# Recurrent branch of a two-block network: gate tiles ahead of its levels, eight pieces a level, banks and tile order of its own

## The reference, cut to what matters

```python
y_a = hgrn2_mixer(hq, hf, hi, hg, lb_all[l], hgrn_norm[l])
y_b = pool_mixer(pz, pool_w[l], pool_scale[l])
y_c = dsa_mixer(sq, sk, sv, iq, ik, iw)
y_m = mem_attention(mq, mk, mv)
merged = None
for bi, y in enumerate((y_a, y_b, y_c, y_m)):
    term = jax.nn.sigmoid(u @ w_gate[l, bi]) * (y @ w_branch[l, bi])
    merged = term if merged is None else merged + term
h = h + rms_norm(merged @ w_out[l], norm_mix_post[l])
```

## Time and profile before

| | us |
|---|---|
| median of 3 runs | 2456.65 (2456.44 to 2456.81) |
| profiled execution | 2457.71, of which the span of the core 2455.9 |
| PE busy | 2274.6 (93% of the span) |
| DVE, ACT, POOL busy | 1263.6, 895.2, 368.3 |
| PE's share of the chain that ended last | 81% |
| mean granted clock of TensorE | 0.957 of full |

### The profile page before, as it was taken

The page is one execution under the profiler, slowest core; times in us unless marked ns, Lnnn a source line. Parts: engine busy times, 40 slices in busy tenths (PEclk is TensorE's granted clock), DMA queues, the critical chain, the costliest instruction groups (busy, mean ns, idle before and its releaser), DMA issues.

```text
span 2455.9 us, 28046 instructions
## 1 busy us (share of the span) xinstructions
PE 2274.6 (93%) x10190; PEld 1767.6 (72%) x10192; DVE 1263.6 (51%) x1966; ACT 895.2 (36%) x1479; POOL 368.3 (15%) x228
## 2 busy tenths in 40 slices
PE   7879799999999999899999888999969897999998
PEld 5646588888776676688888676467658675888886
DVE  4466553243464444642443664268569558443344
ACT  3444443143244453431332453322343233332333
POOL 0000420001320002400003500133022164000001
PEclk9999999999999999999999989879989898999999
DMA  5012133333233232233332332123211131333322
GB/s 163 17 36 65 52 86 103 102 94 96 67 93 107 69 86 69 69 102 103 92 97 81 91 90 71 35 62 98 74 39 56 43 99 52 104 88 107 95 70 77
DMA packets 360224, 196.43 MB, mean 80 GB/s; under 512 B 12575, under 2 KB 355372, under 8 KB 360124
## 3 DMA queue, kind: packets, MB, share of 16 engines
q1 hardware_dynamic: 360124, 195.10, 27.8%
HBM read 192.93 MB, written 2.14 MB: 79 GB/s over the span
## 4 chain that ended last, share of the span: by engine, by line
PE 81%; DVE 10%; ACT 4%; issue 2%; POOL 1%; SPq 1%; DMA 1%; DVEq 0%; ACTq 0%; POOLq 0%
PE PB L393 20%; PE PB L395 20%; PE PB L394 20%; PE PB L1284 3%; PE PB L1286 2%; PE PB L1285 2%; PE PB L494 2%; PE PB L475 2%; PE PB L521 1%; PE PB L1312 1%; PE PB L1361 1%; DVE WL L363 1%; ACT WH L357 1%; PE PB L1269 1%; ACT PR L582 1%
## 5 line engine op out<-in xcount | busy, mean ns | idle before, releaser
L393 PE MATMUL PB<-XH,WH 128*128 128x512 f32 (+1 forms) x1344 | 539.2, 401 | 45.1 <-DVE XL L785 23.2
L394 PE MATMUL PB<-XL,WH 128*128 128x512 f32 (+1 forms) x1344 | 532.0, 396 | 0.0
L395 PE MATMUL PB<-XH,WL 128*128 128x512 f32 (+1 forms) x1344 | 531.4, 395 | 0.0
L357 ACT ACTIVATE WH<-RAW 128x1024 fp32r<-128x1024 f32 (+2 forms) x379 | 380.3, 1007 | 411.3 <-PE PB L395 370.3
L373 DVE TENSOR_TENSOR WL<-RAW,WH 128x1024 fp32r<-128x1024 f32 x192 | 252.5, 1315 | 186.8 <-ACT WH L357 177.0
L393 PEld LDWEIGHTS PB<-XH,WH 128*128 128x128 f32 (+1 forms) x1344 | 257.3, 191 | 106.8 <-issue 48.7
L395 PEld LDWEIGHTS PB<-XH,WL 128*128 128x128 f32 (+1 forms) x1344 | 256.6, 191 | 56.7 <-issue 1.0
L394 PEld LDWEIGHTS PB<-XL,WH 128*128 128x128 f32 (+1 forms) x1344 | 257.3, 191 | 53.3 <-issue 0.8
L363 DVE TENSOR_TENSOR WL<-RAW,WH 128x1024 fp32r<-128x1024 f32 (+3 forms) x135 | 168.7, 1252 | 160.7 <-ACT WH L357 160.4
L395 PE MATMUL PB<-HH,WL 128*128 128x512 f32 x512 | 199.2, 389 | 0.0
L393 PE MATMUL PB<-HH,WH 128*128 128x512 f32 x512 | 199.2, 389 | 0.0
(11 more groups left out here) (485 smaller groups left out, 3582.7 us busy)
## 6 DMA issues: line engine op xcount, KB each, us to landing
RAW<-in_w_up SPq DMA_DIRECT2D x64, 512.0 KB, 4.1
RAW<-in_w_down SPq DMA_DIRECT2D x64, 512.0 KB, 3.8
RAW<-in_w_ffn_gate_up SPq DMA_DIRECT2D x44, 512.0 KB, 3.8
RAW<-in_w_gate SPq DMA_DIRECT2D x32, 512.0 KB, 4.0
RAW<-in_od_w_in SPq DMA_DIRECT2D x24, 512.0 KB, 6.3
RAW<-in_w_in SPq DMA_DIRECT2D x24, 512.0 KB, 4.0
RAW<-in_ple_w_gate SPq DMA_DIRECT2D x16, 512.0 KB, 4.0
RAW<-in_w_ffn_down SPq DMA_DIRECT2D x16, 512.0 KB, 3.9
```

The lines of the kernel that those rows point to most:

```text
L357: act.activation(WH[:, s, 0:nb], RAW[:, s, 0:nb], ACT.Copy).then_inc(hi_done[s], 1)
L393: pe.matmul(PB[b][0:m, 0:n], WH[:, s, k, 0:m], rh[:, kk, :], start=kk == 0, stop=False)
L394: pe.matmul(PB[b][0:m, 0:n], WH[:, s, k, 0:m], rl[:, kk, :], start=False, stop=False)
L395: x = pe.matmul(PB[b][0:m, 0:n], WL[:, s, k, 0:m], rh[:, kk, :], start=False, stop=kk == last)
```

## The change

- PE takes 18 pieces of branch 2 (gates and branches 0 and 1) before the first level, then eight in each of the levels 0 to 6, seven behind level 7's products and seven behind level 8's. The filling goes on into gates (0,0) and (0,1). Gate (0,2) stands before ATT.HV, gate (0,3) after it: five pieces before BONE's products, three behind. After the norm come branches 0 and 1, gate 4, branches 2 and 3, and then gates 5, 6, 7 each with the branch of one before, and branch 7.
- ACT takes the Tanh of gate (2,0) before Exp of level 0, and in each level that of a gate one further on. It writes out its copies (`high_of`) and Tanhs (`last_act`) for branch 0 one by one. The table for Ln is loaded without a Tanh before it.
- DVE merges (2,0) ahead of XX of level 0 and (2,lv+1) at the end of level lv, and waits for the zeroed ATT and the masks only at the first keep.
- Gates of branch 0 use PB0 and PB1 in turn, its branches PB3 and PB4 with a counter `brf`, and the Tanhs four buffers (GTT gets TMP and VT).
- The tiles of branch 0 are loaded in another order: gates 0 to 3, two branch tiles, gate 4, a branch tile, gates 5 to 7, a branch tile.

```diff
-        GTT = (RS, at("GT1", [P, T], F32, arena + 91 * 1024))
+        GTT = (RS, at("GT1", [P, T], F32, arena + 91 * 1024), TMP, VT)
+        G_LAST = {o: N_GATE[0] + n for o, n in enumerate((0, 1, 2, 3, 6, 8, 9, 10))}
+        B_LAST = {o: N_GATE[0] + n for o, n in enumerate((4, 4, 5, 5, 7, 7, 11, 11))}
...
@@ PE: branch_out
+                    if br == 0:
+                        b, n = 3 + o % 2, B_LAST[o]
+                        if o >= 2:
+                            pe.wait_ge(sem["brf"], cnt.value("brf", o - 2))
...
@@ PE: the levels
-                fill = gated(2)
-
-                def level_fill():
-                    for _ in range(9):
+                fill = itertools.chain(gated(2), gate_parts(0, 0), gate_parts(0, 1))
+
+                def level_fill(n):
+                    for _ in range(n):
                         next(fill)
+                level_fill(18)
...
                     if lv < 7:
-                        level_fill()
+                        level_fill(8)
...
-                level_fill()
+                level_fill(7)
...
-                for _ in gate_parts(0, 0):
+                level_fill(7)
+                for _ in gate_parts(0, 2):
                     pass
...
-                for _ in gate_parts(0, 1):
-                    pass
+                third = gate_parts(0, 3)
+                for _ in range(5):
+                    next(third)
                 for pr in range(2):
...
+                for _ in third:
+                    pass
...
                 branch_out(0, 0)
                 branch_out(0, 1)
-                for o in range(2, DT):
-                    for _ in gate_parts(0, o):
-                        pass
-                    branch_out(0, o)
+                last_gate(4)
+                branch_out(0, 2)
+                branch_out(0, 3)
+                for o in range(5, DT):
+                    last_gate(o)
+                    branch_out(0, o - 1)
+                branch_out(0, DT - 1)
...
@@ ACT
+                gate_act(2, 0)
                 level_exp(0)
-                for lv in range(8):
+                for lv in range(7):
                     level_exp(lv + 1)
-                    gate_act(2, lv)
...
+                    gate_act(2, lv + 1)
+                level_exp(8)
+
+                def high_of(k):
+                    n = N_GATE[0] + k
+                    act.wait_ge(loaded[n % 4], 16 * (n // 4) + 16)
+                    act.wait_ge(used[n % 4], n // 4)
+                    nb = blocks_of(n)
+                    act.activation(WH[:, n % 4, 0:nb], RAW[:, n % 4, 0:nb], ACT.Copy).then_inc(hi_done[n % 4], 1)
+
+                def last_act(o):
+                    n, m = G_LAST[o], gate_bank(0, o)
+                    act.wait_ge(used[n % 4], n // 4 + 1)
+                    act.wait_ge(sem["merge"], cnt.value("merge", {0: 22, 1: 23}.get(o, 20 + o)))
+                    act.activation(GTT[o % 4][:], PB[m % 2][:], ACT.Tanh, scale=0.5).then_inc(evac[m % 2], 1)
+                high_of(3)
+                last_act(0)
+                high_of(4)
+                last_act(1)
+                high_of(5)
+                last_act(2)
+                high_of(6)
...
+                last_act(3)
+                high_of(7)
+                high_of(8)
...
@@ DVE: the levels
-                dve.wait_ge(sem["zeroed"], cnt.value("zeroed", "att"))
-                dve.wait_ge(sem["tabb_in"], 32)
                 decay(0)
+                merge(2, 0)
                 for lv in range(9):
                     scale_by(lv)
                     if lv < 8:
                         decay(lv + 1)
+                    if lv == 0:
+                        dve.wait_ge(sem["zeroed"], cnt.value("zeroed", "att"))
+                        dve.wait_ge(sem["tabb_in"], 32)
...
-                    if lv:
-                        merge(2, lv - 1)
+                    if lv < 7:
+                        merge(2, lv + 1)
```

More of the change, by code:

```diff
@@ L94 @@
  topk hsp hg_x hg_prod hg_read hg_e hg_d hg_o hg_small hx mn m2 varb ln_v x_full sum7q pj pj_free memsum cross xsum
- asum ysum yt yo ot_in xt_in z r_tok merge os""".split()
+ asum ysum yt yo ot_in xt_in z r_tok merge os brf""".split()
 def program(nc, known, t):
@@ L841, in gate_bank, with gate_tile @@
         def gate_bank(br, o):
[L842 to L844 removed]
+            return M_GATE[br] + (o if br == 0 else 2 * o)
         def branch_bank(br, o):
[L847 to L848 removed]
             return M_GATE[br] + 2 * o + 1
+        def gate_tile(br, o):
+            return G_LAST[o] if br == 0 else N_GATE[br] + 3 * (o // 2) + 2 * (o % 2)
         def bank_ready(eng, m):
@@ L916, in gate_loads, with gate_load, branch_load @@
                     wb = t["w_branch_2"][0, br].rearrange("(k p) n -> p k n", p=P)
-                    for i in range(4):
-                        loadn(wg[:, :, 2 * i * P:2 * i * P + P], 8, P)
+                    def gate_load(o):
+                        loadn(wg[:, :, o * P:o * P + P], 8, P)
+                    def branch_load(i):
                         s, u = st.slot(0)
@@ L922, in gate_loads @@
                         st.n += 1
-                        loadn(wg[:, :, 2 * i * P + P:2 * i * P + 2 * P], 8, P)
+                    if br == 0:
+                        for o in range(4):
+                            gate_load(o)
+                        branch_load(0)
+                        branch_load(1)
+                        gate_load(4)
+                        branch_load(2)
+                        for o in range(5, DT):
+                            gate_load(o)
+                        branch_load(3)
+                        return
+                    for i in range(4):
+                        gate_load(2 * i)
+                        branch_load(i)
+                        gate_load(2 * i + 1)
                 for c in first[:3]:
@@ L1268, in branch_out @@
                         w = 2 * k + o % 2
-                        pe.matmul(PB[m % 2][:], WH[:, n % 4, w], YHI[br][:, k], start=k == 0, stop=False)
-                        pe.matmul(PB[m % 2][:], WH[:, n % 4, w], YLO[br][:, k], start=False, stop=False)
-                        x = pe.matmul(PB[m % 2][:], WL[:, n % 4, w], YHI[br][:, k], start=False, stop=k == 1)
+                        pe.matmul(PB[b][:], WH[:, n % 4, w], YHI[br][:, k], start=k == 0, stop=False)
+                        pe.matmul(PB[b][:], WH[:, n % 4, w], YLO[br][:, k], start=False, stop=False)
+                        x = pe.matmul(PB[b][:], WL[:, n % 4, w], YHI[br][:, k], start=False, stop=k == 1)
                     if o % 2:
@@ L1972, in second_act @@
                     done(act.activation(ACC[:, 4 + pr], HG[:, pr], ACT.Tanh, scale=0.5), "hg_e", ("g", pr))
-                lin_ready(act, st)
-                act.wait_ge(sem["merge"], cnt.value("merge", 23))
-                m = gate_bank(0, 1)
-                act.activation(GTT[1][:], PB[m % 2][:], ACT.Tanh, scale=0.5).then_inc(evac[m % 2], 1)
                 act.preload_act_table_set(LN_TABLE)
@@ L1988, in merged_high @@
                     done(act.activation(MGH[:, o], MG[:, o], ACT.Copy), "r_hi", ("merged", o))
-                for o in range(2, DT):
-                    gate_act(0, o)
-                    merged_high(o - 2)
-                merged_high(DT - 2)
-                merged_high(DT - 1)
-                st.m += 32
+                merged_high(0)
+                last_act(4)
+                high_of(10)
+                merged_high(1)
+                high_of(9)
+                merged_high(2)
+                last_act(5)
+                high_of(12)
+                merged_high(3)
+                last_act(6)
+                high_of(13)
+                merged_high(4)
+                high_of(11)
+                last_act(7)
+                high_of(14)
+                for o in range(5, DT):
+                    merged_high(o)
+                st.m += 24
                 assert st.n == N_OUT2
```

46 lines of the change are left out of this document (23 added, 23 removed).

## The result

The changed kernel takes **2468.41 us** (median of 5 runs, 2467.70 to 2471.26) against 2456.81 us for the kernel before on the same chip (2456.44 to 2458.99): ratio 1.0048 [1.0037, 1.0059]. It is slower by some 11.6 us, where 2459.0 (2448 to 2466) had been forecast. Its profiled execution took 2471.26 us, with a span of 2469.4.

What follows compares the result with a forecast made beforehand. PE, busy 93% of the span, was taken as the bound, with DVE nearly full in the levels. -11.2 - 3.2 + 10.5 + 4.5 = +0.6, plus 1.9 for the clock, gave 2460.2 profiled, 2459.0 as median; range 2448 to 2466.

Steps and rivals of the forecast that it cites:

- Start: Ahead of level 0: 18 pieces run early, PE's idle time shrinks from 16.9 to 5.7 us, -11.2 us.
- Levels: Levels of branch 2: merge before XX waits for its branch, so PE idles; +10.5 us, bounds 7 to 13.
- off: Time from a level's last product to the branch's completion in the fill: 1.36 + 0.68(lv-1), 1.4 to 4.8 us.
- c: What POOL's subtraction takes from DVE during merge and XX: 0 to 1.07 us, 0.8 used in the sum.
- The last stall: DVE's chain behind level 6 makes PE wait 2.9 us before the last products, those of level 8.
- E: The end of a level's products on PE, from which the level's later times are counted.
- Norm: Head norm: five pieces instead of a whole gate before the first variance matmul, Ln 3.2 us sooner, -3.2 us.
- The end: First output tile: branches (0,6) and (0,7) back to back put the last MGL 13.5 us after its start, +4.5 us.
- Clock: Three stalls of 2.2 to 3 us in or behind the levels, one followed by half clock: +1.9 us.
- Rival (b): Slower by the clock: each stall over 1.4 us from level 3 drops it, +10.6, about 2467; chance 0.22.
- its sign: Test for the slower-clock rival in the levels: it decides once more than two stalls are followed by half clock.
- Rival (a): The stalls in the levels don't come, only 3 us of stall stay: -8.4, 2448; chance 0.25.

Runs made afterwards that it cites:

- the part alone: Kernel before with only the head norm's part: five pieces of gate (0,1) ahead of the sums, its Tanh behind the norm; 2453.47 us, ratio 0.9991.
- the kernel with both edits: Changed kernel with nine pieces a level, ACT's Tanh ahead of Exp, and a gate between the last two branches; 2441.89 us, ratio 0.9944.

## Why the prediction was wrong, point by point

**Start: right.** The wait is 5.64 us (5.7 forecast), and no level waits behind it for the longer way through ACT.

**Levels: the right mechanism, one term too small.** The stall before the level behind level lv was put at off - 2.0 + c, off the branch's place in the fill and c what POOL takes. With the c of the trace (3.42 - 1.21 = 2.2 before level 3; 0.15 before level 4, in merge; 3.39 - 1.21 = 2.2 before level 5; 1.7 before level 6, where the merge's operation took 2.38 us in place of 0.69) the formula gives 2.2, 0.85, 3.6 and 3.8 us. The trace has 2.00, 0.62, 3.33 and 3.52. So off, 2.0 and the durations hold to 0.3 us. Before level 2 it is less good: merge and XX each lose 1.1 us to POOL there, 1.5 us by the formula and 0.87 in the trace. The failed step is "c is what POOL takes from DVE in that piece, 0 to 1.07 us", with c = 0.8 in the sum. Two lines of POOL's timeline in the kernel before show what that 1.07 was:

```profile
1862.52 2.40 POOL L363 TENSOR_TENSOR WL<-RAW,WH 128x1024 fp32r<-128x1024 f32 x1 [0.37 <-ACT WH L357]
1868.80 1.32 POOL L363 TENSOR_TENSOR WL<-RAW,WH 128x512 fp32r<-128x512 f32 x1 [3.88 <-ACT WH L357]
```

EE began at 1868.91, 0.1 us behind a subtraction of a branch tile, which is only 1.32 us long: it was held for nearly all of it. The merge's operation on GT and MG at 1863.71 (1.75 us in place of 0.69) lost as much to a whole tile's subtraction, of which half was over. So neither is a bound for a whole tile's subtraction, whose 2.40 us stood in the same trace. Held nearly from the start, DVE loses 2.2 us to it, and the change makes both engines start on the same event: c was 2.2 before levels 2, 3 and 5 and at level 7, 1.7 before level 6 and 0.15 before level 4. Sum of the levels 15.0 us in place of 10.5, and above the 13 that were its upper end. I also wrote that POOL's operation "may fall into DVE's new waits" and rounded down for it; it does the opposite, as it is released when the wait ends. The Trainium skill (SBUF — State Buffer, Who interferes with whom) says that a DVE instruction with two SBUF inputs contends with a GpSimd one that reads SBUF, and that the later of the two blocks fully. The prediction named the rule, and let it set only the ends 7 and 13 with a block of 1.07 us; the halved subtraction, and the operation on PB that isn't held, agree with the rule as it stands.

**The last stall: too small, and in another place.** 2.9 us were forecast before the products of level 8 for XX; it is 4.64 us, before the second products of level 7. The forecast had left out that these need a bank that level 7's first keep empties. In its own terms, that keep (0.8 us) ends at E + 4.8 + 0.27 + 1.33 + 2.39 + 2.8 + 0.8 + c = E + 12.4 + c, and PE is there at E + 6.12 + 3.59 = E + 9.7. With the c of the trace (XX at 1925.53 took 3.37 us, so 2.2) that is 4.9 us. The place mattered little: at level 8 the forecast's 2.3 us with the same c would be 4.5. Behind this wait PE waits no more in the levels.

**Norm: right in mechanism.** The Ln comes 3.52 us after ACT's Tanhs on HG begin, in place of 6.61; here is ACT's timeline after.

```profile
1963.69 1.15 ACT L2019 ACTIVATE ACC<-HG 128x512 f32<-128x512 f32 x2
1964.86 1.28 ACT L2020 ACT_TABLE_LOAD   x1
1967.21 0.69 ACT L682 ACTIVATE HGB<-PB,EPS 128x512 f32<-128x512 f32 x1 [1.06 <-PE PB L1423]
```

That is 3.1 sooner (3.2 forecast). PE's waits shrink by 2.4 where -3.2 was forecast, and the part alone gave 1.7 to 2.2 us.

**The end: right in mechanism.** The output tile starts at 2014.33, and the last MGL ends 13.3 us later (13.5 forecast, 9.0 before):

```profile
2022.75 4.88 DVE L2740 TENSOR_TENSOR MGL<-MG,MGH 128x512 fp32r<-128x512 f32 x3
```

Of these 4.3 us, 3.2 are idle time; 4.5 had been forecast as idle. I haven't followed where in the tile the other 1.1 us lie.

**Clock: too small.** One stretch of 2 us was forecast; three came, at 1.5 to 1.7 each, 5.0 in sum. The kernel without them (PE kept busy) is 3.9 us faster. Rival (b), 2467 by the clock, is nearest to the result in its number, and its sign came true: more than two of the stalls were followed by half clock. Its price did not: it has 10 us from the clock in the levels, and there are 5. That its number fits is luck, as c supplies the rest. Of the four stalls of 2 us and more, three were followed by half clock; the one of 3.52 us was not.

**The sum redone:** -11.3 at the start, -2.4 in the norm, +15.0 in the levels, +3.2 at the end are +4.5, with +5.2 for the clock in the whole stage 9.7. Against the forecast of +2.5 that is 4.5 more for the levels, 0.8 less gain in the norm, 1.3 less at the end and 3.2 more for the clock; 1.5 of the measured 11.2 remain open. Rival (a), stalls that don't come, was what one more piece a level makes of the change: with it the start's gain stays whole.

## What to carry to other kernels

Before a step is moved on an engine that is nearly full, ask whose completion releases it, and what else that completion releases: two engines that start on one event can meet again and again (here at levels 3, 5 and 7), and what one coincidence in the old trace cost is no bound for it. The bound is the blocker's whole duration. A fill between dependent steps should be a whole number of the units that its consumers wait for (nine pieces a tile here); one piece less drifts the last unit deeper into each fill, and the stall grows level by level. Judge a stall by its idle time and by the clock behind it: matmuls without use, put into waits that can't be removed, gave 3.9 us here in one kernel and 6.9 in another.

## What the runs showed of the hardware

- A DVE operation with both inputs in SBUF stands still for as long as a POOL operation that began before it still runs: 1.21 us become 3.42 beside one of 2.57 us, and 2.31 beside one of 1.46. Operations with one input in PSUM (GT and PB, 0.69 us) ran at full speed beside the same subtraction.
- TensorE's clock fell to 1.2 GHz behind some waits and not others, and their length alone doesn't tell: after a stall of 2.00 us it fell (products at 1874.83, half clock in 1876 to 1880), after 3.52 us (1915.43) it didn't, nor in the kernel with ACT's order alone after 3.53 us. The same stalls differ from kernel to kernel: with half of POOL's subtraction, and with the other order at the end, the one of 3.52 us was followed by half clock, and in the latter the one of 2.00 us was not. Of the stalls of 4.16 us and more in the levels each was followed by half clock. What decides between was not settled. Each fall in the levels cost 1.4 to 1.7 us, or up to 2.9 where it lasted twice as long.
- Gaps cost more than the waits show. In the kernel with both edits the half clock behind the start, the norm and the output tile took 2.8, 2.0 and 1.6 us of the stage; with the start and the norm filled with matmuls the clock was 1.00 over 220 us, the output tile included, though that still waited 3.7 us.
